# Mixer of the second block: DRAM returns, SSM steps and GELU one slot later, two store counters

## What is computed

```python
proj = h @ w_in[l]                      # q, k, v of the attention and u of the SSM
u = proj[..., ATTN_WIDTH + 2 * KV_WIDTH:]
# _s5_mixer
bu = jnp.einsum('lbgh,gph->lbgp', ul, b_bar)                 # the drive
_, states = lax.associative_scan(_ssm_combine, (a, bu), axis=0)
y = jnp.real(jnp.einsum('lbgp,ghp->lbgh', states, c_c)) + d * ul   # the read-out
g = jax.nn.gelu(y)
out = g * jax.nn.sigmoid(g @ w_glu + b_glu)                  # the gate
# second_block
mix = jnp.concatenate([_rmsnorm(attn), _rmsnorm(ssm)], axis=-1)
h_res = h_res + mix @ w_out[l]
h_res = h_res + jnp.square(jax.nn.relu(h2 @ w_up[l])) @ w_down[l]
```

## Time and profile before

| | us |
|---|---|
| median of 3 runs | 3126.59 |
| lowest, highest | 3124.85, 3131.94 |
| the profiled execution | 3131.7 |
| its span | 3129.9 |
| TensorE busy | 3100.3 (99%) |
| VectorE busy | 1839.1 (59%) |
| ScalarE busy | 1475.0 (47%) |
| GpSimd busy | 688.5 (22%) |
| mean granted TensorE clock | 0.998 |

### The profile page before, as it was taken

One profiled execution on the slowest core, in us unless ns is written; L12 is line 12 of the kernel. 1 busy time (PEld: TensorE's weight loads), 2 busy tenths in 40 slices (PEclk: granted clock), 3 DMA queues, 4 the chain that ended last, 5 costly groups with the idle time before them and its releaser, 6 DMA issues.

```text
span 3129.9 us, 45292 instructions
## 1 busy us (share of the span) xinstructions
PE 3100.3 (99%) x16368; PEld 2657.0 (85%) x16368; DVE 1839.1 (59%) x2369; ACT 1475.0 (47%) x2286; POOL 688.5 (22%) x730
## 2 busy tenths in 40 slices
PE   8999999999999999999999999999999999999999
PEld 7888888888888888888888888889978888888887
DVE  6666655555555567665555555567676545555554
ACT  5454644444345545554453544552555434444343
POOL 1422241231411143032314140115020101001010
PEclk9999999999999999999999999999999999999999
DMA  6543555655656554446556565658423555555554
GB/s 240 189 161 144 188 216 191 218 188 188 218 188 217 191 188 151 153 179 218 188 188 219 188 218 188 224 213 282 173 101 143 188 194 190 196 193 192 190 188 162
DMA packets 66640, 598.04 MB, mean 191 GB/s; under 512 B 14320, under 2 KB 24816, under 8 KB 31424
## 3 DMA queue, kind: packets, MB, share of 16 engines
q1 hardware_dynamic: 54912, 588.17, 51.4%
q10 hardware_dynamic: 11184, 5.49, 0.7%
q0 software_dynamic: 400, 2.44, 0.2%
HBM read 577.93 MB, written 18.15 MB: 190 GB/s over the span
## 4 chain that ended last, share of the span: by engine, by line
PE 95%; ACT 2%; DVE 1%; issue 1%; DMA 1%; ACTq 0%; DVEq 0%
PE bank L670 94%; PE bank L772 1%; DMA urow<-us 0%; PE bank L931 0%; PE bank L820 0%; DVE w_lo L1699 0%; ACT w_hi L1199 0%; DMA par<-params 0%; ACT sqj L1224 0%; DVE w_lo L1705 0%; DVE gbuf L2182 0%; ACT prob L1633 0%; DMA u<-urow 0%; DVE sb L2219 0%; ACT act_hi L1548 0%
## 5 line engine op out<-in xcount | busy, mean ns | idle before, releaser
L670 PE MATMUL bank<-xg,w_hi 128*128 128x512 f32 (+1 forms) x4256 | 1432.4, 385 | 3.2 <-DVE w_lo L1705 1.8
L670 PE MATMUL bank<-xg,w_lo 128*128 128x256 f32 (+1 forms) x4064 | 1142.2, 281 | 0.0
L1699 DVE TENSOR_TENSOR w_lo<-raw,w_hi 128x1024 fp32r<-128x1024 f32 x512 | 666.9, 1339 | 456.6 <-ACT w_hi L1210 456.0
L670 PEld LDWEIGHTS bank<-xg,w_hi 128*128 128x128 f32 x4256 | 788.2, 188 | 169.9 <-issue 4.4
L1210 ACT ACTIVATE w_hi<-raw 128x1024 fp32r<-128x1024 f32 x512 | 513.6, 1052 | 618.4 <-PE bank L670 618.3
L670 PEld LDWEIGHTS bank<-xg,w_lo 128*128 128x128 f32 x4064 | 764.5, 188 | 0.9
L670 PE MATMUL bank<-w_hi,act_hi 128*128 128x512 f32 x1920 | 752.7, 392 | 1.8 <-issue 1.0
L670 PE MATMUL bank<-w_hi,act_lo 128*128 128x512 f32 x1920 | 747.8, 389 | 0.0
L670 PE MATMUL bank<-w_lo,act_hi 128*128 128x512 f32 x1920 | 747.4, 389 | 0.0
L1705 DVE TENSOR_TENSOR w_lo<-raw,w_hi 128x1024 fp32r<-128x1024 f32 x510 | 627.2, 1237 | 172.0 <-ACT w_hi L1199 171.1
L1199 ACT ACTIVATE w_hi<-raw 128x1024 fp32r<-128x1024 f32 x514 | 514.5, 1052 | 173.6 <-PE bank L670 146.6
(11 more groups left out here) (344 smaller groups left out, 1994.6 us busy)
## 6 DMA issues: line engine op xcount, KB each, us to landing
raw<-stream SPq DMA_DIRECT2D x260, 2048.0 KB, 7.8
stabs<-ssm_tabs SPq DMA_DIRECT2D x8, 1176.0 KB, 9.7
rdo<-stabs SPq DMA_DIRECT2D x8, 768.0 KB, 6.5
ssm_bc<-smat SPq DMA_DIRECT2D x8, 640.0 KB, 11.8
raw<-stream SPq DMA_DIRECT2D x4, 1024.0 KB, 8.3
stabs<-ssm_f SPq DMA_DIRECT2D x8, 512.0 KB, 10.9
drv<-stabs SPq DMA_DIRECT2D x8, 512.0 KB, 5.7
trig<-stabs SPq DMA_DIRECT2D x8, 408.0 KB, 5.3
```

What stands on the lines that cost most here:

```text
L670: return pe.matmul(o, a, b, start=start, stop=stop, skip_group_check=True)
L1699: dve.tensor_tensor(flat_lo[j][:, 1024 * h:1024 * h + 1024], flat_raw[r][:, 2048 * j + 1024 * h:2048 * j + 1024 * h + 1024], flat_hi[j][:, ...
```

## The change

The order of the SSM's pipeline in the 20 slots is moved by one, from the load back on. `feed` stays in slot i. `feed_back` goes from slot i+1 to i+2, `drive` and `products`, `driving`, `sums` from i+2 to i+3, `read_out` from i+4 to i+5, `y_out` from i+5 to i+6, `y_back` from i+6 to i+7. SyncE's loads of the tables are moved by one step of its loop against the chunks. The three GELU steps go from slots 14, 16, 17 to 15, 17, 18. As two stores can now be in flight, the counter `us_stored` becomes two, one for each buffer of `us`, and the waits on it are rewritten. GpSimd's program is the same, and so is every instruction apart from its place.

```diff
-        us_stored = sem("us_stored")
+        us_stored = [sem(f"us_stored{i}") for i in range(2)]
...
-        GELU_SQ, GELU_TANH, GELU_HIGH = 14, 16, 17
+        GELU_SQ, GELU_TANH, GELU_HIGH = 15, 17, 18
...
-            for s in range(1, 12):
-                if 0 <= s - 2 and s < T2:
-                    sp.wait_ge(bu_done, s - 1)
-                    load_drive(s)
+            for s in range(1, 13):
+                i = s - 1
+                if 0 <= i - 2 and i < T2:
+                    sp.wait_ge(bu_done, i - 1)
+                    load_drive(i)
                 if s % 2 == 1 and s < 10:
                     chunk((s + 1) // 2 + 2)
-                if 0 <= s - 3 and s < T2:
-                    sp.wait_ge(state_ready, s - 2)
-                    load_trig(s)
-                if 0 <= s - 4 and s - 2 < T2:
-                    sp.wait_ge(y_done, s - 3)
-                    load_readout(s - 2)
+                if 0 <= i - 3 and i < T2:
+                    sp.wait_ge(state_ready, i - 2)
+                    load_trig(i)
+                if 0 <= i - 4 and i - 2 < T2:
+                    sp.wait_ge(y_done, i - 3)
+                    load_readout(i - 2)
...
-                if 2 <= s < T2 + 2:
-                    drive(s - 2)
-                if 4 <= s < T2 + 4:
-                    read_out(s - 4)
+                if 3 <= s < T2 + 3:
+                    drive(s - 3)
+                if 5 <= s < T2 + 5:
+                    read_out(s - 5)
...
-                act.dma_start(urow[i].rearrange("s p q -> p s q"), us[i % 2][:]).then_inc(us_stored, 16)
+                act.dma_start(urow[i].rearrange("s p q -> p s q"), us[i % 2][:]).then_inc(us_stored[i % 2], 16)
...
-                act.wait_ge(us_stored, 16 * i + 16)
+                act.wait_ge(us_stored[i % 2], 16 * (i // 2) + 16)
...
+                if 7 <= s < T2 + 7:
+                    y_back(s - 7)
                 if 6 <= s < T2 + 6:
-                    y_back(s - 6)
-                if 5 <= s < T2 + 5:
-                    y_out(s - 5)
-                if 1 <= s < T2 + 1:
-                    feed_back(s - 1)
+                    y_out(s - 6)
+                if 2 <= s < T2 + 2:
+                    feed_back(s - 2)
...
-                    dve.wait_ge(us_stored, 16 * i - 16)
+                    dve.wait_ge(us_stored[i % 2], 16 * (i // 2))
...
-                if 2 <= s < T2 + 2:
-                    products(s - 2)
-                    driving(s - 2)
-                    sums(s - 2)
+                if 3 <= s < T2 + 3:
+                    products(s - 3)
+                    driving(s - 3)
+                    sums(s - 3)
```

## The result

The changed kernel takes 3139.66 us (median of 11 runs, 3137.52 to 3142.10). Beside it the kernel before took 3131.94 us (11 runs, 3124.85 to 3135.96), not the 3126.59 of the first three runs. The ratio is 1.0024, 95% interval [1.0016, 1.0033]: slower by 7.7 us. A second comparison later (the run e12_after_again) gave 3139.94 and 1.0018 [1.0009, 1.0026].

What follows compares the result with a forecast made beforehand. TensorE, busy 99% of the span, was taken as the bound. Savings of 3.0 us plus 0 to 3.4 of clock, against a 4.0 us new wait plus 0 to 3.4, gave +1.0 on 3126.59: 3127.6 us, range 3121.5 to 3133.

Steps and rivals of the forecast that it cites:

- The base: Whole kernel: the predicted difference was laid on the median of 3126.59 us, not on the profiled execution of 3131.7.
- Drive 3's wait goes: Slot 5 of the mixer: TensorE's 2.2 us idle before drive 3 disappears, with 3.4 us to spare.
- SyncE's queue: Weight chunks 3 and 4 and table loads: chunk 3 leaves within 1 us of before; cost 0, at most 2.2 us.
- they are rather earlier: Store and load 3: no later than before, as ScalarE and VectorE are no longer held back in slots 1 to 3.
- sums unchanged: Slots 2 and 12: one loses a drive, the other gains a read-out, total work the same; cost 0.
- The half clock behind it: Mixer, after drive 3's wait: TensorE's half-speed stretch goes with the wait, saving 0 to 3.4 us.
- The 0.35 and the 0.4: Drive 2's delay of 0.35 us and slot 18's wait of about 0.4 us for the key-head copy both go.
- The new wait before the gates: First gate half after slot 19: TensorE waits 4.0 us for the end of the later GELU, `gelu_low`.
- The clock behind it: At the gates, after the new wait: TensorE's clock likely halves, costing 0 to 3.4 us.
- The sum: Whole kernel: all terms together give -2.4 to +4.4 us, middle +1.0.
- The change doesn't do what it says: Rival, chance 0.09: store 3 or a later one lands so late that TensorE still waits; 3129.9 to 3133.3 us.
- What would show it: Signs: no idle before drives, ScalarE's `urow<-us` waits shrink from 27.0 us, 3.5 to 4.5 us idle before the gates.

Runs made afterwards that it cites:

- e12_after_again: The changed kernel itself, timed once more beside the kernel before: 3139.94 us, ratio 1.0018.
- e10: The kernel before with 18 unread matmuls at the end of slot 5's tile, where TensorE waits for load 3: 3131.30 us, ratio 0.9988.
- e1: The changed kernel with the three GELU steps back in slots 14, 16 and 17: 3132.76 us, ratio 1.0002 to the kernel before.
- e7: The changed kernel with 32 unread matmuls just ahead of the gates: 3137.05 us, ratio 1.0012 to the kernel before.
- e6: e1 with 18 unread matmuls at the end of slot 5's tile, ahead of drive 2: 3131.29 us, ratio 0.9990 to the kernel before.
- e2: The kernel before with only the three GELU steps moved to slots 15, 17, 18: 3135.47 us, ratio 1.0009.
- e9: e5 with the three GELU steps in slots 15, 17, 18 as in the change: 3132.72 us, ratio 0.9992 to the kernel before.
- e4: The kernel before with SyncE issuing weight chunk 4 only once store 3 has landed: 3127.81 us, ratio 0.9984.
- e3: e1 with SyncE issuing weight chunk 4 only once load 2 has landed: 3127.81 us, ratio 0.9984 to the kernel before.
- e8: e1 with SyncE issuing weight chunk 3 earlier, ahead of its waits for loads 0 and 1: 3127.97 us, ratio 0.9983 to the kernel before.
- e11: e5 with weight chunk 4 held until store 3 has landed: 3128.10 us, ratio 0.9979 to the kernel before.
- e5: e1 with ScalarE issuing load i right ahead of store i+1 instead of right behind it: 3127.14 us, ratio 0.9979 to the kernel before.

## Why the prediction was wrong

- **The base.** It was laid on 3126.59, the median of three runs. Later groups gave the kernel before 3131.94 to 3134.90. The text said that nothing showed whether the other runs had the profiled one's clock loss, and then took the low median. e10 shows that the loss comes and goes. Of the 12.1 us by which the time was missed, 5.4 are this and 6.7 are the difference of the two kernels, +7.7 instead of +1.0. A difference should have been laid on a base between the two.
- **"Drive 3's wait goes": right by the letter, and no gain.** Drive 3 had time to spare as worked out. The step that failed is "*SyncE's queue* ... I cost these at 0", together with "they are rather earlier". The text noted that slot 2 loses a drive and called the sums unchanged. But by that drive and its scans slot 3's store and split came 3.3 and 3.6 us earlier, while chunk 3 and load 2 stayed. So chunk 4 left 3 us behind chunk 3 instead of 6.6, and store 3 went out ahead of load 2 instead of 2.8 us behind it. Load 2 took 16.8 us instead of 8.0, and drive 2 waited 2.26 us with 5.1 us of clock behind it, where the text had a price of at most 2.2. The drive's 2.0 us stand in the earlier trace rows. I followed transfer 3 and not its neighbour, and checked when each transfer leaves, not beside what it flies.
- **The half clock behind it** did not go but grew, from 3.4 to 5.1 us, in both profiles of the changed kernel (and in those of e1 and e7, which have the same wait). That it is a price of its own was right (e6, e10).
- **The 0.35 and the 0.4** went.
- **The new wait before the gates** was right in place, releaser and size: 4.0 foretold, 3.87 measured. The clock behind it had bounds of 0 and 3.4, with 1.7 in the sum; the traces have 3.0 (after), 1.7 (e2) and 1.5 (e9, e12), and e7 saves 2.6 to 3.8.
- **The sum.** Against its middle values the profile after has +2.2 for the drive's wait (0 instead of -2.2), +3.4 for the clock behind it (+1.7 instead of -1.7), -0.1 for the wait at the gates and +1.3 for the clock there: 6.8, as good as the 6.7 missed.
- **The rivals.** "The change doesn't do what it says" was given 0.09, with a net of 3.3 to 6.7 us over the base. It is the one that came, and for the reason it gives, that chunks 3 and 4 come closer together: store 3 landed after 17.0 us, and what TensorE waited for was load 2 behind it. The measured 7.7 and, the second time, 5.0 us lie on both sides of its upper end: the half clock behind the drive grew, which no case had. The rule that the prediction cites from the Trainium skill ("TensorE: Matmul & The Clock Gate", section on HAM oscillation) held at the gates: the first gate half began or soon went on at half clock in every profile with the wait of 3.9 us there (after, e2, e9, e12) and in none where it was filled (e7).
- **What would show it.** ScalarE's waits for `urow<-us` did shrink, from 27.0 us to 7.9, and TensorE's time did not follow; in e4 they stayed at 26.6 us and TensorE's loss in the slots went. The view had put the trouble on the wrong wait.

## What to carry to other kernels

Giving a late transfer one more stage moves its neighbours too. Before doing so, write down for each small transfer what will be in flight with it and what stands ahead of it on its queue: here one wait ahead of a 2 MB chunk, or the load ahead of the store, was worth 5.7 to 7.4 us, and the extra slot nothing that the runs can tell. Taking a piece of work out of a slot moves up everything behind it in that slot, transfers too. When a chain at the end of a stage moves by one slot, compare its slack with the length of the slot (3.4 against 6.7 us here), and price the clock behind the new wait as well. Where runs of the base differ by more than the effect, three of them are no base.

## What the runs showed of the hardware

- A transfer of 136 KB of the input tiles took 2.3 to 5.7 us in the slots ahead of chunk 3 (before, after). Store 3 took 6.3 to 8.9 us with one chunk of 2 MB beside it (e3, e4, e8, e11) and 12.9 to 17.1 with chunks 3 and 4 beside it (before, after, e1, e5, e9, e12). Table loads of 0.4 to 0.8 MB were in flight as well; beside one chunk and several of them a later store took 12.6 (e4).
- Load 2 took 16.6 to 16.8 us right behind store 3 (after, e1, e12), 8.9 there with chunk 4 held back (e3), and 7.9 to 8.1 ahead of it (before, e5, e9).
- One wait of 2.2 us of TensorE was followed by no half clock (e2), by 6.8 us of it (before) or by 10.2 (after, e12). Behind the same wait of 3.9 us at the gates came 3.4 us (e2, e9, e12) or 6.8 (after). So the loss behind a wait is a range, and it is a good part of what the executions of the kernel before differ by. Why the changed order always showed the longest stretch is open: its runs lie close together, 3137.5 to 3142.1, and no run here tells the reason.
